# Convolution taps shared by two engines, a projection on weights split in advance, norm sums on GpSimd

## What is computed

```python
def conformer_conv(h, pw1, pw1_b, dw, dw_b, ln_g, ln_b, pw2, pw2_b):
    z = h @ pw1 + pw1_b                       # 2048 -> 4096
    z = z[..., :2048] * sigmoid(z[..., 2048:])
    z = causal_dwconv(z, dw) + dw_b           # 31 taps per feature
    z = silu(layernorm(z, ln_g, ln_b))
    return z @ pw2 + pw2_b                    # 2048 -> 2048

def sq_relu_mlp(h, w1, w2):                   # 2048 -> 8192 -> 2048
    a = relu(h @ w1)
    return (a * a) @ w2

x = x + even_mixer(rmsnorm(x, e_norm), ...)   # layer 0
x = x + sq_relu_mlp(rmsnorm(x, f_norm[0]), f_w1[0], f_w2[0])
x = x + conformer_conv(rmsnorm(x, o_norm), ...)   # layer 1
x = x + sq_relu_mlp(rmsnorm(x, f_norm[1]), f_w1[1], f_w2[1])
return rmsnorm(x, final_norm)
```

## Time and profile before

| | before |
|---|---|
| median of 3 runs | 2259.25 us (2258.96 to 2260.84) |
| the profiled execution: time | 2260.48 us |
| its span, first to last instruction | 2258.7 us |
| TensorE, matmuls | 2169.3 us, 96% of the span |
| VectorE | 1552.5 us, 69% |
| ScalarE | 969.8 us, 43% |
| GpSimd | 11.5 us, 1% |
| read from HBM, written | 393.49 MB, 2.10 MB |
| mean granted TensorE clock | 0.989 of full speed |

### The profile page before, as it was taken

How to read it: one execution, slowest core, us unless ns; L and a number is a source line. 1 busy time by engine, 2 the same in 40 slices (tenths; PEclk the granted TensorE clock), 3 DMA queues, 4 the chain that set the end, 5 groups by cost and what they waited for, 6 DMA issues and landing times.

```text
span 2258.7 us, 35712 instructions
## 1 busy us (share of the span) xinstructions
PE 2169.3 (96%) x13974; PEld 2007.9 (89%) x13974; DVE 1552.5 (69%) x1795; ACT 969.8 (43%) x1034; POOL 11.5 (1%) x25
## 2 busy tenths in 40 slices
PE   7998998899999999999999999899999999999996
PEld 7988898899999999999998888788899999999995
DVE  7667657567756756756774999977665765765765
ACT  4544344444544544544551100264544544544553
POOL 0000000000000000000000000000000000000000
PEclk9999999999999999999999999999999999999998
DMA  6434224445555555555553444244455555555553
GB/s 222 176 113 139 96 110 131 150 177 187 205 205 202 190 203 204 198 195 205 202 198 137 150 153 159 79 149 188 185 205 198 193 204 204 195 196 204 203 196 120
DMA packets 55862, 396.82 MB, mean 176 GB/s; under 512 B 6496, under 2 KB 6880, under 8 KB 8544
## 3 DMA queue, kind: packets, MB, share of 16 engines
q1 hardware_dynamic: 54288, 389.32, 47.8%
q0 software_dynamic: 1488, 6.29, 1.0%
HBM read 393.49 MB, written 2.10 MB: 175 GB/s over the span
## 4 chain that ended last, share of the span: by engine, by line
PE 75%; DVE 15%; issue 4%; ACT 3%; DMA 2%; DVEq 0%; ACTq 0%; SPq 0%; POOL 0%
PE ps L1023 40%; PE ps L1025 20%; DVE work L918 4%; DVE wlo L577 4%; PE ps L1050 4%; PE ps L1109 3%; PE ps L998 3%; PE ps L1002 3%; PE ps L1000 2%; DMA raw<-in_wts 2%; ACT whi L277 2%; DVE sq_part L617 1%; DVE work L684 0%; PE ps L1104 0%; DVE work L768 0%
## 5 line engine op out<-in xcount | busy, mean ns | idle before, releaser
L577 DVE TENSOR_TENSOR wlo<-raw,whi 128x1024 fp32r<-128x1024 f32 x672 | 817.3, 1224 | 496.8 <-ACT whi L277 483.5
L277 ACT ACTIVATE whi<-raw 128x1024 fp32r<-128x1024 f32 x672 | 706.3, 1057 | 713.9 <-PE ps L1025 368.3
L1023 PE MATMUL ps<-hid,whi 128*128 128x512 f32 x2304 | 755.8, 382 | 5.8 <-DVE hid L951 3.3
L1023 PE MATMUL ps<-xg,whi 128*128 128x512 f32 x2048 | 674.6, 383 | 6.8 <-ACT sq_part L322 4.5
L1025 PE MATMUL ps<-hid,wlo 128*128 128x256 f32 x2304 | 628.0, 273 | 0.0
L1025 PE MATMUL ps<-xg,wlo 128*128 128x256 f32 x2048 | 559.4, 273 | 0.0
L1023 PEld LDWEIGHTS ps<-hid,whi 128*128 128x128 f32 x2304 | 435.4, 189 | 68.0 <-issue 3.9
L1023 PEld LDWEIGHTS ps<-xg,whi 128*128 128x128 f32 x2048 | 388.3, 190 | 62.4 <-ACT sq_part L322 5.1
L1025 PEld LDWEIGHTS ps<-hid,wlo 128*128 128x128 f32 x2304 | 442.4, 192 | 0.0
L1025 PEld LDWEIGHTS ps<-xg,wlo 128*128 128x128 f32 x2048 | 394.5, 193 | 0.0
L998 PE MATMUL ps<-xg,whi 128*128 128x256 f32 x768 | 221.6, 289 | 11.6 <-DVE wlo L577 11.6
(11 more groups left out here) (194 smaller groups left out, 1405.1 us busy)
## 6 DMA issues: line engine op xcount, KB each, us to landing
raw<-in_wts SPq DMA_DIRECT2D x368, 1024.0 KB, 4.8
x<-in_xt SPq DMA_DIRECT2D x4, 512.0 KB, 8.2
x<-in_xt POOLq DMA_DIRECT2D x1, 2048.0 KB, 9.9
out_t<-work POOLq DMA_DIRECT2D x4, 512.0 KB, 3.3
work<-in_rows POOLq DMA_DIRECT2D x12, 128.0 KB, 3.9
ct<-in_consts SPq DMA_DIRECT2D x1, 768.0 KB, 6.2
work<-in_w_s POOLq DMA_DIRECT2D x4, 128.0 KB, 4.4
dwt<-in_dw SPq DMA_DIRECT2D x1, 248.0 KB, 5.2
```

Source lines behind the costliest of these rows:

```text
L277: nc.scalar.activation(whi[:, i % SPLIT].rearrange("p a b -> p (a b)"), raw[:, r, HALF * (i % 2):HALF * (i % 2) + HALF], ACT.Copy).then_in ...
L577: tt(wlo[:, i % SPLIT].rearrange("p a b -> p (a b)"), raw[:, i // 2 % RAW, HALF * (i % 2):HALF * (i % 2) + HALF], whi[:, i % SPLIT].rearra ...
L1023: mm(ps[:, 4 * par + n, :], whi[:, r, k, cols], woven_parts(operand[:, kt]), start=(kt == 0), stop=False)
```

## The change

Four things change.

First, the taps. A tile now is the unit, 16 of them. ScalarE makes the products of taps 0 to 23 (`tap_products`, three blocks of eight tiles of 256, in a ring of four blocks `prods` that lies in the space of `hid`), VectorE adds the blocks (`add_blocks`), folds eight products to one (`fold`) and adds it to its own sum of taps 24 to 30 (`tap`, `add_folds`). The adds for tile g-1 stand between the taps of tile g.

Second, the first projection goes tile by tile (`pw1_group`: one value and one gate tile), with three f32r matmuls of 256 columns per kt on split weights, as in `narrow_group`. The split is made during the first MLP: in each of its 32 groups two halves of `pw1` are loaded (`pre_load`), split (`pre_high_part`, `pre_low_part`) and stored to memory (`pre_store`, hi and lo, 512 KB each). SP waits for all stores and then loads hi and lo straight into the four slots (`pw_load`).

Third, the sums for the LayerNorm: GpSimd adds the pivot to tiles 0 to 7, and adds up tiles and squares 0 to 14; TensorE sums only these two tiles and the last one.

Fourth, smaller moves: tile 15's two last squares come behind four high parts and an early Sqrt on ScalarE, and of the four low parts that VectorE made ahead of the mean two now stand behind the first normalized block. `UNSPLIT` is renamed `APART`, and the sixteen tiles are written out without a loop.

The core of the diff:

```diff
+            def pre_load(p, half, count):
+                sp.wait_ge(pre_low, count)
+                sp.dma_start(pre_raw[:, p, :], pw1[half]).then_inc(pre_in[p], 16)
+            def pre_store(p, half, count):
+                sp.wait_ge(pre_low, count)
+                sp.dma_start(pw_hi[half], pre_hi[:, p, :].bitcast(F32)).then_inc(pre_hi_out[p], 16)
+                sp.dma_start(pw_lo[half], pre_lo[:, p, :].bitcast(F32)).then_inc(pre_lo_out[p], 16)
...
+            with sp.Fori(0, PW_HALVES // 2 - 1) as g:
+                split_chunk(2 * g + 2 * G_MLP0 + 3, 0)
+                pre_load(0, 2 * g, 2 * g + 1)
+                split_chunk(2 * g + 2 * G_MLP0 + 3, 1)
+                pre_load(1, 2 * g + 1, 2 * g + 2)
+                split_chunk(2 * g + 2 * G_MLP0 + 4, 0)
+                split_chunk(2 * g + 2 * G_MLP0 + 4, 1)
+                pre_store(0, 2 * g, 2 * g + 3)
+                pre_store(1, 2 * g + 1, 2 * g + 4)
...
+            for p in range(2):
+                pre_load(p, PW_HALVES - 2 + p, PW_HALVES - 1 + p)
+            for p in range(2):
+                pre_store(p, PW_HALVES - 2 + p, PW_HALVES + 1 + p)
+            for p in range(2):
+                sp.wait_ge(pre_hi_out[p], 16 * (PW_HALVES // 2 + 1))
+                sp.wait_ge(pre_lo_out[p], 16 * (PW_HALVES // 2 + 1))
...
+            def pw_load(half, r):
+                sp.dma_start(whi[:, r].rearrange("p a b -> p (a b)").bitcast(F32), pw_hi[half]).then_inc(pw_hi_in[r], 16)
+                sp.dma_start(wlo[:, r].rearrange("p a b -> p (a b)").bitcast(F32), pw_lo[half]).then_inc(pw_lo_in[r], 16)
+            for r in range(SPLIT):
+                sp.wait_ge(half_free, 8 * G_PW1 + r + 1)
+                pw_load(r, r)
+            with sp.Fori(1, KT) as g:
+                for r in range(SPLIT):
+                    sp.wait_ge(pw_used, SPLIT * g + r - SPLIT + 1)
+                    pw_load(SPLIT * g + r, r)
...
+            pool.wait_ge(s["conv"], 2)
+            nc.gpsimd.memset(ln_sum, 0.0).then_inc(s["ln_sums"], 1)
+            nc.gpsimd.memset(ln_sum_sq, 0.0).then_inc(s["ln_sums"], 1)
+            pool.wait_ge(s["pivot"], 1)
+            for t in range(PIVOT_TILE):
+                pool.wait_ge(s["conv"], t + 1)
+                nc.gpsimd.tensor_tensor(conv[:, t, :], conv[:, t, :], pivot, ALU.add).then_inc(s["pivoted"], 1)
+            for t in range(KT - 1):
+                if t < PIVOT_TILE:
+                    pool.wait_ge(s["pivoted"], t + 1)
+                else:
+                    pool.wait_ge(s["conv"], t + 1)
+                pool.wait_ge(s["ln_sums"], t + 2)
+                nc.gpsimd.tensor_tensor(ln_sum, ln_sum, conv[:, t, :], ALU.add).then_inc(s["ln_sums"], 1)
+                pool.wait_ge(s["ln_sq"], t + 1)
+                if t:
+                    pool.wait_ge(s["sq_used"], t)
+                nc.gpsimd.tensor_tensor(ln_sum_sq, ln_sum_sq, ln_squares[:, t % 2, :], ALU.add).then_inc(s["sq_used"], 1)
...
+            def pre_high_part(q, j, p):
+                act.wait_ge(pre_in[p], 16 * (8 * q + j + 1))
+                act.wait_ge(pre_hi_out[p], 16 * (8 * q + j + 1))
+                copy(pre_hi[:, p, :], pre_raw[:, p, :]).then_inc(pre_high, 1)
...
+            def tap_products(g):
+                act.wait_ge(s["z_new"], g + 1)
+                for b in range(BLOCKS):
+                    n = BLOCKS * g + b
+                    if n >= RING:
+                        before, part = divmod(n - RING, BLOCKS)
+                        act.wait_ge(s["blocks"], (BLOCKS - 1) * before + max(part, 1))
+                    for i in range(BLOCK_TAPS):
+                        k = BLOCK_TAPS * b + i
+                        dst, w = prods[:, n % RING, i, :], dwt[:, g, k:k + 1]
+                        if k:
+                            ins = nc.scalar.activation(dst, window(g, k), ACT.Copy, scale=w)
+                        else:
+                            ins = nc.scalar.activation(dst, window(g, k), ACT.Identity, scale=w,
+                                                       bias=param("dw_b")[:, g:g + 1])
+                    ins.then_inc(s["prods"], 1)
...
+            for g in range(KT):
+                gate(g)
+                tap_products(g)
+                if g == PIVOT_AT:
+                    act.wait_ge(s["pivot_sum"], 1)
+                    nc.scalar.activation(pivot, ps[:, 7, 0:T], ACT.Copy, scale=-1.0 / (2 * P)).then_inc(s["pivot"], 1)
+                if PIVOT_TILE <= g < 14:
+                    square(2 * (g - PIVOT_TILE))
+                    square(2 * (g - PIVOT_TILE) + 1)
+                elif g >= 14:
+                    square(g - 2)
+            act.wait_ge(pw_used, PW_HALVES)
             for i in range(4):
-                high_part(G_PW2, i, UNSPLIT)
-            squares(6, slice(12, 14))
-            squares(7, slice(14, 16))
+                high_part(G_PW2, i, APART)
+            nc.scalar.activation(flat_small[:, 0:1], eps, ACT.Sqrt)
+            square(14)
+            square(15)
...
+            def pre_low_part(q, j, p):
+                dve.wait_ge(pre_high, 16 * q + 2 * j + p + 1)
+                dve.wait_ge(pre_lo_out[p], 16 * (8 * q + j + 1))
+                tt(pre_lo[:, p, :], pre_raw[:, p, :], pre_hi[:, p, :].bitcast(F32), ALU.subtract).then_inc(pre_low, 1)
...
+            def add_blocks(g, b):
+                dve.wait_ge(s["prods"], BLOCKS * g + b + 1)
+                if b > 1:
+                    dve.wait_ge(s["blocks"], (BLOCKS - 1) * g + b - 1)
+                tt(folds, block_of(g, 0) if b == 1 else folds, block_of(g, b), ALU.add).then_inc(s["blocks"], 1)
...
+            for g in range(KT):
+                par = 2 * (g % 2)
+                dve.wait_ge(pw_used, 4 * g + 4)
+                tt(halves(total[:, par:par + 2, :]), in_order(ps[:, par:par + 2, 0:T]), halves(by_token(rms[:], 2)),
+                   ALU.mult).then_inc(s["glu_scaled"], 1)
+                if g:
+                    add_blocks(g - 1, 1)
+                gated(g)
+                tap(g, 0)
+                if g:
+                    add_blocks(g - 1, 2)
+                tap(g, 1)
+                if g:
+                    fold(g - 1, 4)
+                tap(g, 2)
+                if g:
+                    fold(g - 1, 2)
+                tap(g, 3)
+                if g:
+                    fold(g - 1, 1)
+                tap(g, 4)
+                if g:
+                    add_folds(g - 1)
+                tap(g, 5)
+                tap(g, 6)
+            add_blocks(KT - 1, 1)
+            add_blocks(KT - 1, 2)
+            for n in (4, 2, 1):
+                fold(KT - 1, n)
+            add_folds(KT - 1)
+            low_part(G_PW2, 0, APART)
+            low_part(G_PW2, 1, APART)
...
             normalize(0)
+            low_part(G_PW2, 2, APART)
+            low_part(G_PW2, 3, APART)
...
+            def pw1_group(g):
+                par = 2 * (g % 2)
+                if g < 2:
+                    pe.wait_ge(banks_free, G_PW1 + 1)
+                else:
+                    pe.wait_ge(s["z_new"], g - 1)
+                for r in range(SPLIT):
+                    if g == 0 and r == 3:
+                        mean_squares(2, G_PW1)
+                    if g == PIVOT_AT and r == 2:
+                        pe.wait_ge(s["conv"], 2)
+                        pe.wait_ge(root_ready, 3)
                         for t in range(2):
                             ins = mm(ps[:, 7, 0:T], const("ones"), conv[:, t, :], start=(t == 0), stop=(t == 1))
                         ins.then_inc(s["pivot_sum"], 1)
-                    r = kc % RAW
-                    pe.wait_ge(raw_in[r], 16 * (2 * G + kc // 2 + 1))
-                    if norm is not None:
-                        pe.wait_ge(xg_raw, 4 * norm + kc + 1)
-                    for k in range(CH_K):
-                        kt = CH_K * kc + k
-                        for n in range(4):
-                            ins = mm(ps[:, 4 * par + n, 0:T], raw[:, r, CH_N * k + P * n:CH_N * k + P * n + P],
-                                     xf[:, kt, :], start=(kt == 0), stop=(kt == KT - 1))
-                    ins.then_inc(raw_used, 1)
+                    pe.wait_ge(pw_hi_in[r], 16 * (g + 1))
+                    pe.wait_ge(pw_lo_in[r], 16 * (g + 1))
+                    if g == 0:
+                        pe.wait_ge(xg_ready, 9 + r)
+                    hi, lo = (w[:, r].rearrange("p a b -> p (a b)") for w in (whi, wlo))
+                    for k in range(4):
+                        kt = 4 * r + k
+                        for n in range(2):
+                            dst, cols = ps[:, par + n, 0:T], slice(2 * P * k + P * n, 2 * P * k + P * n + P)
+                            mm(dst, hi[:, cols], woven(xg[:, kt, 0, :]), start=(kt == 0), stop=False)
+                            mm(dst, hi[:, cols], woven(xg[:, kt, 1, :]), start=False, stop=False)
```

(20 more changed lines are left out.)

303 lines of the change are left out of this document (152 added, 151 removed).

## The result

The changed kernel takes 2314.99 us (median of 4 runs, 2313.93 to 2316.91) against 2259.6 us of the kernel before in the same session: a ratio of 1.0245, 95% interval 1.0228 to 1.0263. It is 55 us slower; 2236 was forecast, and the time lies outside the range of 2227 to 2266. The profiled execution has a span of 2312.1 us, 53.4 more than the 2258.7 of before.

| stretch | before | after | difference |
|---|---|---|---|
| start to the end of the first MLP (TensorE's last matmul of it) | 1199.3 | 1265.8 | +66.5 |
| from there to the second projection's first matmul | 268.8 | 255.3 | -13.5 |
| from there to the end | 790.6 | 791.0 | +0.4 |

The account below looks back on a forecast made before the run. It took TensorE to bound the first MLP, and TensorE and VectorE the first projection with its convolution. 2260.5 - 24.1 (projection stage) + 1.0 (second projection) = 2237.4, as a median about 2236 us; range 2227 to 2266.

Parts of the forecast that it names:

- 10.7 us per tile for TensorE: First projection: 96 matmuls of 256 columns at 0.111 us each make a tile, against 13.9 us before.
- ScalarE's pace of 0.40 per product: First projection: one tap product of 256 elements every 0.40 us, 24 products 9.8 us per tile.
- The projection's gap: Start of the first projection: TensorE idle 22 us for last low parts, stores and loads; low clock loses 2.3 us more.
- Who sets the pace: First projection: ScalarE becomes the bound, 11.0 us per tile at first, later 11.8; VectorE 0.1 to 0.9 below it.
- Margin 2.2 us; cost 0: First MLP: a weight chunk lands 5.8 us into the next group, may come at 8.0, so added transfers cost nothing.
- 6 x 2.62 + 1.06 + 1.23: First MLP: time after the previous group's end, put at 18.2 us, when the low part freeing the chunk's slot is done.
- Rival (C): First MLP: DMA engines can't carry the traffic, deciding under 337 GB/s; at 320 GB/s total 2295 us; chance 0.14.
- (B): First projection's stage: GpSimd's adds hold VectorE up, 11 to 15 us, total 2249 us; chance 0.26.
- The bounds of 0 and 11 us: GpSimd's 38 new adds: 0 if beside all else, 11 if VectorE stands still 0.43 us for each, less slack.
- The upper figure of 15 us: Loss from GpSimd's 38 adds if each takes about 0.65 us, estimated from the skill's cycles per element.
- Rival (D): First projection waits for weights: 4.19 MB per tile at 357 GB/s, 0.7 us over in eight tiles; 2242 us; chance 0.07.
- (E): First projection: ScalarE's products beside VectorE take 0.49 us each instead of 0.40, total 2271 us; chance 0.05.

Follow-up runs that it names:

- e2: Changed kernel with GpSimd's 30 adds into the norm's sums left out (semaphores and the 8 pivot adds kept): 2307.3 us, ratio 1.0216.
- e5: Changed kernel with each 1 MB raw weight load cut into two half loads, each waiting only for its own half: 2244.1 us, ratio 0.9943.
- e6: As e5, with the pre-splitting's loads and stores also spread, at most one behind each of a group's first six half loads: 2222.1 us, ratio 0.9842.
- e7: Changed kernel with whole chunks but without the first MLP's stores of split halves (projection's result left out): 2248.0 us, ratio 0.9949.
- e1: Changed kernel with a group's two stores moved behind the next group's first and second weight chunks: 2322.5 us, ratio 1.0286.
- e11: As e6, with pre-splitting one group earlier, tile 0's weights loaded as slots free, and squares summed by TensorE matmuls: 2196.9 us, ratio 0.9724.

## Why the prediction was wrong

**The engines' prices held.** 10.7 us per tile for TensorE: the first scaled tiles follow each other in 10.6 and 10.8 us. ScalarE's pace of 0.40 per product: 17 in 6.90 us. A tile without GpSimd took 11.37 us (e2), where 11.8 was forecast. The projection's gap: 24.3 us against 22, at half the granted clock for the first 5 us, as forecast. From the end of the sixteenth gated tile to the second projection: 35.2 us (1485.9 to 1521.1) against 35.7. Ten matmuls behind GpSimd's last add took 6.5 us against 6.6, with VectorE idle for 4.32 us in front of the mean.

**Who sets the pace was half wrong, and luck hid it.** ScalarE was to be the bound from the first tile on, with 11.0 us, and TensorE "no longer the bound". In the first tiles the pace is TensorE's: the chain that ended last between 1300 and 1360 us runs through its matmuls for 82.5%, and ScalarE waits 0.6 to 2.0 us per tile for the gated tile. From the first gated tile to the sixteenth 170.7 us were forecast; without GpSimd's sums they are 170.4 (e2). But the first eight intervals there took 91.1 us instead of 88.5, among them one of 12.2 and one of 13.0, and the last seven 79.3 instead of 82.2. The agreement of the sum is partly luck.

**The step that failed is "Margin 2.2 us; cost 0"** in the paragraph on the first MLP. It asked how late one chunk may come, once, in a group that otherwise runs at 21.0 us. But the slot is a ring: a chunk that comes late is split late, and the next load is issued late. What has to be under 21.0 us is the sum of two loads and two splittings. The rest of that loop, without the load behind the stores, takes 15.9 us in the trace above (23.3 - 7.4), and 14.6 and 15.8 in the two rounds before it. With the prediction's own 6.6 us for that load (20.2 to 5.8 us into the next group) a group comes to 21.2 to 22.5 us: up to 1.5 us over in each of 31 groups, up to 46 us of loss without any limit of rate. The load was too short as well: between 700 and 800 us it took 7.4 to 8.3 us, and the loss is 66.5. e5 and e6 bear this out: shorten the loop, and with the same bytes the loss is gone; e7 fits it too. Two of the prediction's sums are off without deciding anything: 6 x 2.62 + 1.06 + 1.23 is 18.0 and not 18.2, and tile 0 would end at 1221.6 + 10.7 + 2.3 = 1234.6 and not at 1235.4.

**Rival (C) had the outcome and the wrong mechanism.** It put the place right (stores in front of the next chunk) and named 2295, but made it a matter of rate, decided at 337 GB/s. The engines carried 351 GB/s in e6. The 318 to 324 GB/s in the changed kernel are not the cause but the result: a group of 7.34 MB in 23 us. Its chance of 0.14 was too small because I tested only the rate and one chunk's lateness. That its 2295 lies near the result is luck.

**GpSimd was priced at 0, and (B) was true.** The bounds of 0 and 11 us held it: 7.7 us of the whole (e2), 10.3 of the stage. Taking the lower end rested on TensorE and ScalarE reading the same memory beside VectorE without slowing it, which says nothing of GpSimd. In three stretches of the stage, forecast and measured: to the first gated tile 38.3 and 40.0 us, from there to the sixteenth 170.7 and 180.1, from there to the second projection 35.7 and 35.2. Together that is 244.7 against 255.3, so 13.5 us were won instead of 24.1. The middle one is 170.4 without the sums, 9.7 less; 1.2 of these 9.7 are a tile that waited for its weights in the changed kernel and not in e2. The Trainium skill, "SBUF — State Buffer", on the ports that VectorE and GpSimd share, calls them "an exclusive lock, not a bandwidth split". The rows above fit that: the block sum that starts at 1448.73, while an add runs to 1449.40, takes 2.82 us instead of 2.28, and the add that starts at 1449.36 ends at 1452.14, behind the block sum's end at 1451.55. The upper figure of 15 us rested on about 0.65 us per add, an estimate from the Trainium skill, "GPSIMD Engine Reference", side-by-side cycle accounting. That page's 2.6 cycles per element at its clock of 1.2 GHz give 0.55 us by themselves, and the prediction doesn't say what the other 0.1 is. With 0.65 its own sum would be 38 x 0.65 - 5 = 20 us, not 15. An add took 0.91 us.

**Rival (D) came for one microsecond.** TensorE waited once for split weights, 0.97 us at 1329.05, and that tile came 1.2 us late (11.93 us instead of 10.75 in e2). Nothing like 0.7 us in each of eight tiles came, for the DMA engines carried more than the 357 GB/s that (D) took (columns as in the earlier trace rows):

```profile
1300.00:1400.00 100.00, 99.03 (x881) 98.71 (x880) 88.99 (x121) 85.92 (x209) 8.37 (x9) 1.00 1.00 381
```

The Trainium skill, "DMA: Bandwidth & Descriptors", specifications, gives about 358 GB/s as a core's HBM limit, half of what two cores share; this kernel runs on one core, this stretch of 100 us is above that figure, and the measurement decides. (E) did not come: the pace of the products was 0.40.

## What to carry to other kernels

When a change adds transfers beside a stage, don't ask only for the rate and for one transfer's slack: write down each buffer's round trip (load, every step until it is free, the next load), count its rounds per period, and compare the sum with the period. If it doesn't fit, cut the buffer's unit of reuse in two before adding memory (51 us in the first MLP here), and put at most one foreign transfer between two loads (18 more). The sum is a first test and no forecast to the microsecond, as a load's landing time moves with what else is under way. Adds on GpSimd beside a full VectorE cost VectorE when they fall on its long operations (38 of them in the changed kernel); one per tile between short operations cost nothing in e11, and neither did the matmuls with ones on TensorE.

## What the chip showed that I had not expected

The cutting of loads paid even without the change: two loads of 512 KB that wait for their own halves make the kernel before 0.9% faster (2239.05 us), and land in 4.1 us (median) instead of 4.8. Landing times under load grow well before the DMA engines are full: between 700 and 920 us a 1 MB chunk took 4.7 us (median) in the kernel before at a share of 0.56, 5.0 in e7 at 0.68, 6.5 in the changed kernel at 0.88, and 7.0 in e1 at 0.84. One add of 256 f32 on GpSimd took 0.91 us, against VectorE's 0.43.
